# Two sliding-attention stages of a fused transformer program: the order around the last gate unit, and where the output weights' sums stand

## The reference

```
q, k, v, z = split(u @ w_in)                  # 16 query heads and 4 key heads of 64, gate z of 1024
q, k = rope(rmsnorm(q)), rope(rmsnorm(k))
s = einsum('bnqhgd,bnkhd->bnhgqk', qb, kk) * 64 ** -0.5     # blocks of 128 queries, own and previous block of keys
s = where(band & valid, s, -inf)              # 0 <= distance < 128
m = maximum(s.max(-1), sink)
e = exp(s - m)
p = e / (e.sum(-1) + exp(sink - m))
o = einsum('bnhgqk,bnkhd->bnqhgd', p, vv)
return (o * silu(z)) @ w_out
```

## Time and profile before

| | |
|---|---|
| median of 3 runs | 3493.91 us (3492.92 to 3494.03) |
| the profiled execution | 3494.4 us, of which the span is 3492.6 us |
| busy: PE, DVE, ACT, POOL | 3389.7, 1922.3, 705.3, 234.3 us |
| granted TensorE clock, mean over the span | 0.987 of full speed |
| gate unit 7 starts in the first of the two stages, in the second | 2064.24 us, 3369.61 us |

### The profile page before, as it was taken

One profiled execution on the slowest core, in us unless ns is written; L12 is line 12 of the kernel. 1 busy time (PEld: TensorE's weight loads), 2 busy tenths in 40 slices (PEclk: granted clock), 3 DMA queues, 4 the chain that ended last, 5 costly groups with the idle time before them and its releaser, 6 DMA issues.

```text
span 3492.6 us, 43761 instructions
## 1 busy us (share of the span) xinstructions
PE 3389.7 (97%) x16603; PEld 2692.3 (77%) x16603; DVE 1922.3 (55%) x4402; ACT 705.3 (20%) x1667; POOL 234.3 (7%) x362
## 2 busy tenths in 40 slices
PE   8989999999999999999999999999999999999998
PEld 3475788888855678888888867888887888887866
DVE  4463467554404564675545668543365656557566
ACT  2221021100014540211101143022212011121152
POOL 0000000000002330000000032000010000000042
PEclk9999999999999999999999999999999999999999
DMA  3201312222210013122222221222222222102211
GB/s 134 76 21 37 121 49 86 95 85 85 109 65 33 13 49 121 49 85 85 86 96 85 86 74 37 85 73 71 75 82 63 100 75 85 47 13 99 96 63 49
DMA packets 43206, 256.38 MB, mean 73 GB/s; under 512 B 5918, under 2 KB 9146, under 8 KB 14848
## 3 DMA queue, kind: packets, MB, share of 16 engines
q1 hardware_dynamic: 31616, 224.41, 17.7%
q0 software_dynamic: 6896, 17.34, 1.8%
q10 hardware_dynamic: 4496, 11.91, 1.3%
HBM read 242.81 MB, written 2.18 MB: 70 GB/s over the span
## 4 chain that ended last, share of the span: by engine, by line
PE 57%; DVE 3%; issue 1%; ACT 1%; DMA 0%; POOL 0%; ACTq 0%; POOLq 0%; DVEq 0%
PE PL L1303 19%; PE PX L1303 14%; PE PL L985 6%; PE PL L1675 4%; PE PL L1497 2%; PE PX L1786 2%; PE PL L969 1%; PE PL L1700 1%; PE PL L1829 1%; PE PL L1584 1%; ACT SCR L2301 1%; PE PL L1570 1%; DVE SCR L3153 1%; DVE SCR L3189 0%; PE PL L1055 0%
## 5 line engine op out<-in xcount | busy, mean ns | idle before, releaser
L985 PE MATMUL PL<-xn,ring 128*128 128x264 f32 (+1 forms) x1584 | 490.2, 467 | 11.0 <-DVE xn L2538 10.5
L985 PEld LDWEIGHTS PL<-xn,ring 128*128 128x128 f32 x1584 | 300.0, 191 | 187.0 <-issue 154.8
L1303 PE MATMUL PL<-Z,ring 128*128 128x256 f32 (+1 forms) x1200 | 286.7, 390 | 10.1 <-DVE Z L3604 8.6
L2599 DVE TENSOR_TENSOR Z<-PL,SCR 128x512 f32<-128x512 f32 (+3 forms) x104 | 63.8, 613 | 409.0 <-PE PL L985 323.3
L1303 PEld LDWEIGHTS PL<-Z,ring 128*128 128x128 f32 x1200 | 232.5, 194 | 48.0 <-DVE Z L3604 9.8
L1303 PE MATMUL PL<-AUX,ring 128*128 128x256 f32 (+1 forms) x1104 | 255.6, 380 | 0.0
L1303 PEld LDWEIGHTS PL<-AUX,ring 128*128 128x128 f32 x1104 | 209.7, 190 | 29.2 <-DVE AUX L2943 0.2
L1303 PE MATMUL PL<-xn,ring 128*128 128x264 f32 (+1 forms) x864 | 199.9, 383 | 1.2 <-DVE xn L2841 1.2
L1303 PEld LDWEIGHTS PL<-xn,ring 128*128 128x128 f32 x864 | 163.9, 190 | 28.1 <-DVE xn L2841 1.5
L1974 ACT ACTIVATE SCR<-PL 128x256 f32<-128x256 f32 (+1 forms) x72 | 27.6, 383 | 733.8 <-PE PL L1303 733.8
L1303 PE MATMUL PX<-Z,AUX 128*128 128x264 f32 (+1 forms) x704 | 165.5, 386 | 2.7 <-DVE Z L3413 2.7
(11 more groups left out here) (553 smaller groups left out, 6028.0 us busy)
## 6 DMA issues: line engine op xcount, KB each, us to landing
ring<-w_tiles SPq DMA_DIRECT2D x212, 1024.0 KB, 4.8
Z<-Z ACTq DMA_DIRECT2D x16, 264.0 KB, 5.3
SCR<-head_rows POOLq DMA_DIRECT2D x16, 264.0 KB, 3.7
AUX<-norm_scratch POOLq DMA_DIRECT2D x8, 528.0 KB, 7.2
cst<-consts ACTq DMA_DIRECT2D x1, 2205.5 KB, 15.2
AUX<-SCR POOLq DMA_DIRECT2D x8, 264.0 KB, 4.6
resid<-x ACTq DMA_DIRECT2D x4, 512.0 KB, 9.0
Z<-norm_scratch POOLq DMA_DIRECT2D x4, 512.0 KB, 7.3
```

Source lines behind the costliest of these rows:

```text
L985: mm = pe.matmul(PL[:, 2 * h + c, 0:e - a], ring[t % 2][:, k, P * h:P * h + P], src_block(name, k)[:, a:e], start=k == 0, stop=k == KB - 1)
L1303: mm = pe.matmul(ps, lhs(k), rhs(k), start=kc == 0 and k == 0, stop=kc == per - 1 and k == 3)
L2599: ins = dve.tensor_tensor(d, ps, f, ALU.mult)
```

## The change

In each of the two stages the order of four things is different. PE issues the scores of group 5 between the halves of gate unit 7 rather than after the whole unit. ACT does the exponentials of group 5 and the copy of the transposes of group 4 ahead of opening the last gate. DVE does `bias_max(5)` and `normalise(4)` ahead of copying that unit out of PSUM, and the loops of ACT and DVE then begin at group 5. The weight sums of the output layer move from passes 4 and 5 of the DVE loop to passes 12 and 13. No operation is added or removed.

```diff
@@ pe: window @@
                 values(3)
                 scores(4)
-                gate_part(7, 0, KB)
+                gate_part(7, 0, 4)
                 scores(5)
+                gate_part(7, 4, KB)
                 pe.wait_ge(psum_free, evacuated(n + "_z"))
@@ act: window @@
                 exps(4)
+                exps(5)
+                turned(4)
                 open_gate(7)
-                for m in range(N_FIRST_TILE, N_W):
+                for m in range(N_FIRST_TILE + 1, N_W):
                     if m + 1 < N_W:
                         exps(m + 1)
                     turned(m)
@@ dve: window @@
                 outputs(3)
                 bias_max(4)
+                bias_max(5)
+                normalise(4)
                 copy_out(n + "_z", 7)
-                for m in range(N_FIRST_TILE, N_W):
+                for m in range(N_FIRST_TILE + 1, N_W):
                     if m + 1 < N_W:
                         bias_max(m + 1)
                     normalise(m)
-                    if m > N_FIRST_TILE:
-                        outputs(m - 1)
-                    if m in (4, 5):
-                        weight_sums(n + "_out", 0, m - 4)
+                    outputs(m - 1)
+                    if m in (12, 13):
+                        weight_sums(n + "_out", 0, m - 12)
                 outputs(N_W - 1)
```

## The result

| | before | after |
|---|---|---|
| median | 3494.03 us (3492.42 to 3497.63, 13 runs) | 3501.73 us (3498.32 and up, 13 runs) |
| ratio after / before | | 1.0021, 95% interval 1.0013 to 1.0028 |
| the profiled execution, its span | 3494.4, 3492.6 us | 3502.17, 3500.4 us |
| granted clock, mean of the span | 0.987 | 0.986 |

The changed kernel is 7.3 us slower (0.0021 of 3494), just over the 0.2% that the prediction had set as the mark of a real difference, and outside the predicted range of 3491.0 to 3498.5 us. One run of 4267.77 us at a clock of 0.78 is left out of the ratio.

The account below looks back on a forecast made before the run. TensorE, busy 97% of the span, was taken as the bound. Order -3.95, sums +4.1 and one clock fall +1.5 gave +1.6 us on 3494.4: 3496.0 profiled, 3495.5 us median, range 3491.0 to 3498.5.

Parts of the forecast that it names:

- -3.95, +4.1 and +1.5: Both stages together, in us: won by the new order, lost to the moved weight sums, lost to one clock fall.
- The order: Around gate unit 7: the new order puts the loop 2.3 us ahead in the first stage, 1.65 in the second.
- the stand: PE idle 3.0 us between `scores(8)` and `values(5)`, waiting for ACT's queue behind `turned(4)`.
- two table loads in a row: ACT between `turned(4)` and `exps(6)`: 2.56 us by the rows; 5.3 by the page, a rival at 3499.5 us, 2%.
- I expect one fall in the two stages together, +1.5 us.: PE's new stand before `values(5)` brings the clock down to 1.2 GHz once in two stages; own case, 43%.
- a second, weaker occasion: At group 13: the sums hold PE up by 2 us, which might also bring the clock down.
- The third rival: Clock falls at the new stand in both stages and behind the sums, +4.5 to +6, 3498.5 to 3500 us; 13%.
- no fall at all: Rival at the new stand: PE's wait is too short to lower the clock; +0.15, 3494.1 us; 25%.
- With 2.05 us of sums [...] `turn(13)` ends 1.9 to 2.0 us late.: Group 13: sums before `bias_max(14)` delay the loop; 2.05 us a stage taken, 4.1 for two.
- costs nothing: The fourth addition, one group later, falls where DVE waits for `values(13)`; 0.6 us if that cover is gone.
- The ring: Loop of turn, copy to SBUF, values, turn: closed, so a late `turn(13)` puts off all that follows.
- The rival that the sums are absorbed: The ring catches up at 16-row groups 16 to 19, or sums cost half; 3490 to 3492 us, 15%.

Follow-up runs that it names:

- e2: Changed kernel with the weight sums back in their old place (behind copy_out 7 and in pass 5), so the new order alone; 0.9987 to the kernel before.
- e5: Changed kernel plus unread matmuls in PE's waits, six before `values(5)` and five before `turn(13)` in each stage; 1.0005 to the kernel before.
- e4: Kernel before, old order, with both parts of the weight sums behind `bias_max(4)`, where DVE waits for gate unit 7; 0.9984 to the kernel before.
- e1: Kernel before, old order, with only the weight sums moved to passes 12 and 13; 1.0005 to the kernel before.
- e8: Changed kernel with `open_gate(7)` ahead of `turned(4)` and the weight sums early, in DVE's waits ahead of copy_out 7; 3482.95 us, 0.9973 to the kernel before.
- e6: Changed kernel with the four additions of the weight sums spread one by one over passes 9 to 12; 1.0012 to the kernel before.
- e10: e8 with one part taken back, `turned(4)` again ahead of opening the last gate on ACT; 3491.38 us, 0.9992 to the kernel before.
- e3: Changed kernel plus six unread matmuls in each stage, in PE's stand before `values(5)` only; 1.0016 to the kernel before.
- e9: Changed kernel with the weight sums in passes 16 and 17, the short groups, instead of 12 and 13; 1.0005 to the kernel before.
- e7: Changed kernel with only ACT's order altered, `open_gate(7)` ahead of `turned(4)`; 1.0005 to the kernel before.

## Why the prediction was wrong, point by point

**The ledger.** At full clock and with the sums covered the two stages take twice e2's 64.3, that is 128.6 us, 4.3 under the 132.9 of before. The holds add 5.6 (e5, 134.2), the falls of the clock 6.0 (140.1): +7.2 us, but for rounding. The prediction had -3.95, +4.1 and +1.5.

**The order, right in its times.** `turn(4)` came in one piece, `turned(4)` started at 2075.90 for the 2075.75 forecast, the copy cost PE 0.80 for 0.8, `values(5)` started at 2083.35 for 2083.3, and the stand was 3.13 for 3.0. Its 3.95 us stand against 4.3 in the ledger. By the two table loads in a row the Trainium skill, "ScalarE: Activation LUTs", What ACT_TABLE_LOAD costs, would have put `values(5)` an estimated 2.8 us later; the loads took 1.28 each, and what followed began within 0.02 us of their ends. The rows had decided that rightly.

What the prediction did not see is whose gain this is. It added up the two parts as if each had a price of its own. But the 4.3 us come from taking the additions out of `turn(4)`'s way, and the old order has them too when the sums are covered (e4: 63.9 us a stage without a fall, e2: 64.3). On top of sums moved to 12 and 13 (e1) the new order costs 2.7 us in the two stages. Only with the gate opened ahead of `turned(4)` is a stage shorter than e4's (e8: 62.3).

**The failed step: "I expect one fall in the two stages together, +1.5 us."** There were three, 6.0 us by e5. I had reasoned that the new stand was shorter and in one piece. The runs show that a stand of 3.13 us in that place is followed by a fall in six stages of eight, and the hold at `turn(13)`, called "a second, weaker occasion", in seven of eight, so that it is no weaker. The price of a fall, 1.5 us, held in the first stage and was too low in the second, by the little that the old order's second stage had lost. There `values(5)`, `turn(6)` and `scores(9)` take 5.80 us from start to start of the `values` in place of 3.29, 2.5 us more, and `values(13)` and `turn(14)` 1.6 more. Three falls at 2.0 us on average stand against one at 1.5. The third rival, falls at both stands and behind the sums, was the right one, with 13%; it said 3498.5 to 3500 us, and 3501.7 lies beyond it, because its three falls cost 6.0 us and not 4.5, and because of the second step below. Its opposite, no fall at all, had 25% and came true only where idle matmuls filled both places (e5) or the waits were shortened (e8).

**The second step that failed in size: "With 2.05 us of sums [...] `turn(13)` ends 1.9 to 2.0 us late."** Against the loop's own place it ended 2.9 us late (2.8 a stage by e5), so the sums cost 5.6 us in place of 4.1. Two things were left out, and both are one mechanism. The 2.0 us were read off, where POOL is the one that loses time (2.82 us in place of 1.35); in the new place the sums meet POOL's product with the gate, DVE loses too, and they take 2.39. And the fourth addition, "costs nothing", finds no wait of DVE for `values(13)`: it stands behind the copy of group 12, runs beside `normalise_upper(13)`, and makes it 1.86 us in place of 1.35, which PE now waits for. The Trainium skill, "SBUF — State Buffer", SBUF: two separate sides, has it that of such a pair the one that starts first holds the port for its whole instruction, and the other stands. The rows agree both ways, in round numbers: POOL's product of 0.73 us takes 1.16 behind the first addition, and the second addition of 0.68 takes 1.21 behind that. I had drawn from the rule only that POOL would be late.

**The ring, right.** The short groups take back only 0.25 us: 2.89 are lost up to `scores(16)`, and 2.64 are left at the first product (1.79 behind the kernel before, and 0.85 ahead of it at `turn(12)`, 2106.25 against 2107.10). The rival that the sums are absorbed fell: e1, e5 and e6 all keep them.

**Not seen: the sums were free elsewhere.** In the new order DVE has gaps ahead of the gate's copy. With the sums there or right behind the copy no hold appears (e2, e8, e10), and the old order has room for them as well (e4). The prediction took their 2 us as a cost that had to stand somewhere.

**What stays open.** Outside the two stages the profiled executions differ by up to 3.9 us with the same instructions, e.g. 3359.7 us before (3492.6 - 132.9) and 3360.3 after, but 3356.6 in e8 and 3360.5 in e3. How often each of the three falls comes in an execution is known from single profiles only, and several of them are longer than their kernel's median (e1 by 2.6 us, e3 by 1.9, e10 by 3.4); the ratios are of many executions and carry the sum of it. Why one and the same stand is followed by a fall in one stage and not in another is not shown.

## What to carry to other kernels

Work inserted into a loop that closes as a ring costs its length there, and what it and its neighbour lose by running side by side; put it where its engine waits for something else, and read that wait before choosing. Do not price the parts of a change one by one and add them up: here each part alone was harmless (e1, e2), and together they cost 7.3 us. When a change makes the main engine stand for some microseconds, price the fall of its clock behind each such place, and take it as likely, not as an occasion. Filling the waits with idle matmuls is a cheap experiment that separates the wait's own length from the clock behind it.

## What the runs showed of the hardware

- The same stand does not always bring the clock down. A stand of 3.13 us in front of `values(5)` was followed at once by work at 1.2 GHz in both stages of the kernel after and of e10 and in the second stage of e9; in e6's first stage only from `turn(6)` on (1.86 us); and not at all in the first stage of e9 and the second of e6. The stand of 2.73 us in e2 was followed by a fall in the first stage and by none in the second. The Trainium skill, "TensorE: Matmul & The Clock Gate", Part 1, calls the monitor's window free-running; these rows agree with that.
- Behind the hold at `turn(13)`, 2.05 to 2.22 us for DVE and up to 0.6 for POOL, the clock fell in seven of the eight stages that had it unfilled (the kernel after, e1, e3, e7), not in the first stage of the kernel after. Behind e6's holds of 0.3 to 1.0 us for DVE it never fell.
- Eleven matmuls that compute nothing of use, in two stands a stage, made the program 5.6 us faster.
